# Fewer sample slots in the recurrent, state, norm and key stages, more of them in the prompt heads

## What is computed

```python
for layer in range(DEPTH):
    xp = half_ffn(xp, norm_g[layer, 0], *ffn_a)
    xd = half_ffn(xd, norm_g[layer, 0], *ffn_a)
    hp = rms_norm(xp, norm_g[layer, 1])
    hd = rms_norm(xd, norm_g[layer, 1])
    if layer % 2 == 0:      # ab_mixer: attention heads and recurrent heads, concatenated
        yp, ckv_p, kpe_p, sp = ab_mixer(hp, cos_p, sin_p, s0_p, attend_p, *shared)
        yd, ckv_d, kpe_d, sd = ab_mixer(hd, cos_d, sin_d, state_hgrn[j], attend_d, *shared)
    else:                   # c_mixer: a short gated convolution
        ...
```

## Time and profile before

| | |
|---|---|
| median of 3 runs | 2304.62 us (2302.82 to 2311.08) |
| the profiled execution | 2304.24 us |
| its span, first to last instruction | 2302.5 us |
| mean granted TensorE clock | 0.97 of full speed |
| PE busy | 2189.5 us (95%) |
| DVE, ACT, POOL busy | 1033.1, 750.2, 119.9 us |
| HBM read, written | 255.29 MB, 5.16 MB |

### The profile page before, as it was taken

The page is one execution under the profiler, slowest core; times in us unless marked ns, Lnnn a source line. Parts: engine busy times, 40 slices in busy tenths (PEclk is TensorE's granted clock), DMA queues, the critical chain, the costliest instruction groups (busy, mean ns, idle before and its releaser), DMA issues.

```text
span 2302.5 us, 46795 instructions
## 1 busy us (share of the span) xinstructions
PE 2189.5 (95%) x18285; PEld 2078.3 (90%) x18285; DVE 1033.1 (45%) x1994; ACT 750.2 (33%) x1305; POOL 119.9 (5%) x226
## 2 busy tenths in 40 slices
PE   7999999998777878999999999999999999999997
PEld 7999999997443557999999999999999999999997
DVE  5444344366653343544443444443346664444333
ACT  5222232464222432522222342222232234222222
POOL 0000000001134331000000000000000000000000
PEclk9999999998886897999999999999999999999998
DMA  4222233234799972222223222222322222222231
GB/s 151 91 91 91 91 101 100 83 128 134 210 271 277 248 204 71 92 92 91 91 91 101 101 92 91 91 90 93 99 94 91 91 93 92 91 91 91 92 101 65
DMA packets 100014, 261.98 MB, mean 114 GB/s; under 512 B 14386, under 2 KB 47171, under 8 KB 99843
## 3 DMA queue, kind: packets, MB, share of 16 engines
q1 hardware_dynamic: 88722, 228.83, 31.6%
q0 software_dynamic: 11184, 31.69, 4.7%
HBM read 255.29 MB, written 5.16 MB: 113 GB/s over the span
## 4 chain that ended last, share of the span: by engine, by line
PE 61%; DVE 1%; ACT 1%; issue 0%; DVEq 0%; ACTq 0%
PE bank L276 20%; PE bank L275 20%; PE bank L277 20%; PE bank L1845 0%; PE bank L1828 0%; PE bank L1859 0%; PE bank L1834 0%; ACT sb_prob L826 0%; DVE sb_prob L1314 0%; DVE sb_x L1435 0%; PE bank L1620 0%; PE bank L293 0%; DVE sb_x L362 0%; ACT L301 0%; ACT L298 0%
## 5 line engine op out<-in xcount | busy, mean ns | idle before, releaser
L275 PE MATMUL bank<-sb_h_hi,sb_w_hi 128*128 128x260 f32 x3552 | 1007.3, 284 | 15.2 <-DVE sb_w_lo L252 12.0
L276 PE MATMUL bank<-sb_h_lo,sb_w_hi 128*128 128x260 f32 x3552 | 1007.9, 284 | 0.0
L277 PE MATMUL bank<-sb_h_hi,sb_w_lo 128*128 128x260 f32 x3552 | 1004.6, 283 | 0.0
L246 ACT ACTIVATE sb_w_hi<-sb_raw 128x1024 fp32r<-128x1024 f32 x339 | 359.0, 1060 | 1239.4 <-PE bank L277 1237.7
L275 PEld LDWEIGHTS bank<-sb_h_hi,sb_w_hi 128*128 128x128 f32 x3552 | 669.4, 188 | 17.7 <-DVE sb_w_lo L252 12.0
L277 PEld LDWEIGHTS bank<-sb_h_hi,sb_w_lo 128*128 128x128 f32 x3552 | 672.3, 189 | 0.0
L276 PEld LDWEIGHTS bank<-sb_h_lo,sb_w_hi 128*128 128x128 f32 x3552 | 669.0, 188 | 0.2
L252 DVE TENSOR_TENSOR sb_w_lo<-sb_raw,sb_w_hi 128x1024 fp32r<-128x1024 f32 x339 | 415.0, 1225 | 379.1 <-ACT sb_w_hi L246 378.2
L276 PE MATMUL bank<-sb_a_lo,sb_w_hi 128*128 128x260 f32 x1408 | 399.1, 283 | 0.0
L275 PE MATMUL bank<-sb_a_hi,sb_w_hi 128*128 128x260 f32 x1408 | 398.5, 283 | 0.0
L277 PE MATMUL bank<-sb_a_hi,sb_w_lo 128*128 128x260 f32 x1408 | 397.7, 282 | 0.0
(11 more groups left out here) (262 smaller groups left out, 1576.3 us busy)
## 6 DMA issues: line engine op xcount, KB each, us to landing
sb_raw<-in_w SPq DMA_DIRECT2D x339, 512.0 KB, 3.5
sb_s_raw<-in_cache SPq DMA_DIRECT2D x256, 144.0 KB, 4.9
sb_v_raw<-in_cache POOLq DMA_DIRECT2D x192, 128.0 KB, 5.6
sb_v_raw<-in_cache SPq DMA_DIRECT2D x64, 128.0 KB, 6.1
sb_x<-in_x SPq DMA_DIRECT2D x4, 520.0 KB, 6.3
out_y<-sb_x SPq DMA_DIRECT2D x8, 260.0 KB, 2.2
sb_st<-in_state POOLq DMA_DIRECT2D x8, 256.0 KB, 7.3
out_state_s<-sb_st POOLq DMA_DIRECT2D x8, 256.0 KB, 5.3
```

What stands on the lines that cost most here:

```text
L246: nc.scalar.activation(w_hi[slot][:], raw[slot][:], ACT.Copy).then_inc(S("w_hi_done"), 1)
L275: nc.tensor.matmul(out, wh, xh, start=first and c == 0, stop=False)
L276: nc.tensor.matmul(out, wh, xl, start=False, stop=False)
L277: mm = nc.tensor.matmul(out, wl, xh, start=False, stop=last and c == chunks - 1)
```

## The change

It changes five functions and adds a row of constants and one more, nothing else. Slots up to 20 stay where they are.

```diff
+PROMPT_SLOTS_IN = PROMPT_STEPS - 8
...
+        HGRN_SLOTS, STATE_SLOTS, NORM_SLOTS, KV_SLOTS = 54, 60, 68, 78
+
         def after_hgrn(m, part):
-            return 4 * m + part + 1
+            n = 4 * m + part + 1
+            return n if n <= LAG else LAG + (n - LAG) * (HGRN_SLOTS - LAG) // (4 * HG - LAG)
 
         def after_state(u):
-            return 65 + u + 1
+            return HGRN_SLOTS + (u + 2) * (STATE_SLOTS - HGRN_SLOTS) // (BATCH_D + 1)
 
         def after_norm(n):
-            return 73 + n + 1
+            return STATE_SLOTS + n * (NORM_SLOTS - STATE_SLOTS) // 9
 
         def after_kv(s):
-            return 84 + s
+            return NORM_SLOTS + (s + 1) * (KV_SLOTS - NORM_SLOTS) // 12
 
         def after_prompt(t):
-            return 96 + (t + 1) * (SLOTS - 96) // PROMPT_STEPS
+            return min(SLOTS, KV_SLOTS + (t + 1) * (SLOTS - KV_SLOTS) // PROMPT_SLOTS_IN)
```

## The result

The change takes 2309.91 us (median of 13 runs, 2303.88 to 2314.83), the kernel before 2304.45 in the same comparison (2295.03 to 2311.08): a ratio of 1.0027, interval 1.0014 to 1.0039. That is 5.5 us slower where 4.3 us faster was forecast. It lies inside the range and within the 0.5% that the prediction called "same", but the interval excludes a ratio of 1, so the sign is wrong.

A forecast was written before the change was run, and what follows sets the result against it. DMA transfers, 8.3 us a quad at 268 GB/s, were taken as slightly tighter than compute in the mixer. Terms -7.8 - 16.8 + 28.7 - 8.4 gave -4.3 us, from 2304.6 to 2300.3, range 2287 to 2312.

The forecast's parts named there:

- same: Whole kernel: outcome within 0.5%, 11.5 us, of the kernel before; chance 0.61, against 0.28 faster and 0.11 slower.
- I: Recurrent blocks 5 to 15, 89.8 us before: ten slots and three quads fewer, -8 us, between -4 and -14.
- III: Prompt heads up to the last scores quad, 65.4 us before: +28.7 us to 94.1, between +16 and +35.
- IV: Rest of the prompt heads, 56.1 us before: ten steps already done, -8 us, between -5 and -11.
- the start: Kernel up to the first scores quad of the blocks: no difference forecast, 0 us.
- II: States, norm and keys, 90.0 us before: earlier state loads and fewer slots, -17 us, between -9 and -22.
- V: From the last head's result to the output projection: no difference forecast, 0 us.
- rival (b): Prompt heads: PE runs at half clock, deciding below 0.8 or so in III; +29 us, 2329; chance 0.10.
- The term of 1.45 us for each block without quads: Recurrent blocks: two blocks without quads take 5.0 us instead of 6.45, saving 2.9 us together.
- The state loads: End of block 15: loads of states 2 and 3 issued about 2 us behind the outputs, state steps 8.2 us earlier.
- (a): Prompt heads bound by compute, not transfers: III +17 us or little more, sum -16, 2289; chance 0.25.
- (c): Nothing moves: III takes whole what I and II save, one queue of transfers; 2304.6 us; chance 0.15.

The follow-up runs named there:

- fifth: The changed kernel with a third of the score and half of the value matmuls left out in three quads of four from slot 79: 2311.94 us against 2304.12, 1.0027.
- sixth: The changed kernel with the quads of slots 23 and 39 put behind their block's outputs: 2310.33 us against 2304.12 for the kernel before, 1.0027.
- eighth: The changed kernel with constants 64, 70, 78, 88 (seven slots moved) and state loads first: 2291.87 us against 2304.12 for the kernel before, 0.9942.
- ninth: The changed kernel with constants 64, 70, 78, 88 and state loads first, run again: 2290.47 us against 2303.33 for the kernel before, 0.9954.

## Why the prediction was wrong, step by step

- **What bounds**: right. I and III were close to both limits, and the page rate of 268 GB/s held: 257 to 270 GB/s in every III with full pages whose row stands here.
- **III, the step that failed**: "With full rings at the start, eleven quads must be fetched meanwhile: 11 x 8.3 = 91.3." The rings were not full: the last quad of the key stage (slot 75) stands 8.7 us ahead of the first of the heads, its buffers are loaded again only from 747.3 on, and by then the key stage, with quads every 8.6 us at share 1.06, kept the DMA engines full. So the pages of slot 83 had to come in during III as well: twelve quads, 12 x 8.3 = 99.6, and with the first 2.4 us 102.0 against the 103.3 measured and the 94.1 forecast. Executions with less work or a higher clock took 101.5 and 98.1 for the same twelve. That is 7.9 of the 9.3 us by which III missed. III also lies outside its bounds (+38.0 for +35 at most). The other terms nearly cancel: I and IV came 3.5 and 4.9 us too long and the start 1.4, II and V 4.5 and 3.6 too short. The error was visible beforehand: the prediction itself gave II's transfers "it fits, barely", and what fits barely hands on no full ring.
- **Clock in III**, rival (b): 0.77, under its threshold of 0.8, and the intervals averaged 8.4 us, under its 8.9. It shared in the loss, but by 2 to 5 us at most (the fifth and sixth runs), probably since a slow PE hides most of its time in waits for transfers that it would have had. PE's waits for `in_cache` were therefore 6.1 us in the change and not 10 or more.
- **I**: -4.3 for -7.8, at the small end of its bounds, and as small as the spread between executions. The term of 1.45 us for each block without quads took PE's time for the block's: the two such blocks took 6.2 and 6.1 us and not 5.0, and the waits for DVE grew from 11.7 to 18.1 us. Two of the three quads between outer products and outputs had no part in it (sixth run).
- **II**: -21.3 for -16.8, inside the bounds. The state loads came as forecast, 7.8 us earlier for 8.2. How II and III share their 172.1 us is not independent: what II gains by consuming quads early, III pays. The forecast summed them as if they were, +11.9 for the pair; measured +16.7.
- **IV**: -3.5 for -8.4, outside its bounds. The cadence of 0.83 us a step was taken at a clock of 0.81, and the change had 0.74: PE was busy 42.9 us for 57 steps, 42.5 for 67 before. V: -3.6 for nothing, at clocks of 1.00 and 0.50; it reads 7.2 and 3.8 at the same two clocks in two executions of one kernel (eighth and ninth), so it need not be an effect of the change.
- **Rivals**: (a) fell (half the bytes gave 20 us, less work for PE none). (c), what I and II save III takes whole, was nearest in time (2304.6), but not in its parts: I and II save 25.6, III takes 38.0. Its picture, one queue of transfers up to the last scores, fits; but the idle share of I is 0.26 x 85.7 = 22 us, where 5 were idle before and 16 were forecast, and IV gave 3.5 and not 8.

## What to carry to other kernels

Where transfers run behind a ring of fixed depth, treat the stretch from the first full share to the last as one queue: a transfer moved later leaves the DMA engines idle where it was, and costs its full length, 8.3 us a quad here, as soon as the later stage has no idle time of theirs. Before counting on full rings at a stage's start, look up when the last buffers ahead of it come free, and whether their transfers can land by then once the stage before has itself been made faster. A change of order that comes along with moved work (here the state loads freed of six value loads) can be tried alone: here it gave 2.2 us alone and 12 to 13 with seven slots moved.

## What the runs showed of the hardware

- One kernel's executions differ along with PE's clock. The eighth and ninth runs are the same kernel; profiled at 2303.57 (well above its median of 2291.87) and 2289.61 they show IV as 51.4 us at 0.82 and 47.5 at 0.93. The eighth:
```profile
844.80:896.20 51.40, 41.00 (x290) 29.26 (x291) 21.59 (x66) 17.88 (x50) 13.40 (x25) 0.82 0.39 123
```
  So a few microseconds of a stretch in one profile prove nothing; the medians above do.
- More waiting did not mean a lower clock. III of the sixth run has 14.4 us of PE waits for transfers at 0.91, of the change 6.1 us at 0.77, of the fifth 18.8 at 0.77. The Trainium skill (TensorE: Matmul & The Clock Gate, "HAM oscillation — how this bites in real kernels") has work between DMA waits that outlast it start at half clock; by these three, total waiting does not tell which execution does.
- With a clock of 0.77 in place of 0.91 a stretch bound by transfers took 103.3 us in place of 98.1 (III of the change and of the sixth run), though PE's busy time was 13 us longer.
- The end of the mixer, V, was 3.8 us at a clock of 1.00 and 7.2 to 7.4 at 0.50, in executions of one kernel too.
- Two rings of 128 and 144 KB pages gave 264 to 274 GB/s in the windows of these runs at a share of 1.06 to 1.08. The Trainium skill (DMA: Bandwidth & Descriptors, Specifications) gives about 358 GB/s as a core's limit from HBM. By that page twelve quads would be an estimated 75 us; the fifth and sixth runs took 101.5 and 98.1.
